# Passages between phases done by halves of the tokens, without GpSimd

## The chip, the cores and the metric

One core of a Trainium2 chip. The metric is the device time of one execution in microseconds (us). Five engines work in parallel, each through its own queue in order: TensorE (PE, matmul), VectorE (DVE), ScalarE (ACT), GpSimd (POOL) and SyncE (SP), which only issues DMAs here. They wait for each other through semaphores.

## The reference

A two-layer trunk over 544 tokens: 512 of a prompt and 8x4 of decoding samples, model width 1024. Cut to what matters:

```
def rms_norm(x, g):
    return x * rsqrt(mean(x * x, axis=-1) + EPS) * g

for l in range(DEPTH):                       # DEPTH = 2
    h = rms_norm(x, norm_mix_pre[l])
    if l % 2 == 0: mix = mixer_ab(h, ...)    # short convolution and window attention
    else:          mix = mixer_c(h, ...)     # HGRN2: gated recurrence, 8 heads
    x = x + rms_norm(mix, norm_mix_post[l])
    h = rms_norm(x, norm_ffn_pre[l])
    fo = (gelu(dwconv(h @ w_a)) * (h @ w_b)) @ w_down
    x = x + rms_norm(fo, norm_ffn_post[l])
```

So behind every mixer and every FFN two norms follow each other, over all 1024 channels: the statistics of the phase's output, the residual add, the statistics of the new x, and the scaled h that the next projection multiplies.

## The kernel before

Channels lie on the 128 partitions: x, h and the phase output (`mix`) are 8 tiles (`KD`) of 128 channels by 544 tokens. A PSUM accumulator (`acc[0]`, `acc[1]`) holds one output tile as two halves of 272 tokens (`H`). Each product is made in three passes: each weight and each activation is split into a high and a low part (`w_hi`, `w_lo`, `h_hi`, `h_lo`), and hi·hi, hi·lo, lo·hi are added.

There are eight phases in `PHASES`: in_ab, out_ab, up0, down0, in_c, out_c, up1, down1. Each consists of units, a unit being the weights of one output tile (8 or 11 k-tiles; a tile of down takes two units of 11). A unit's raw weights come by DMA from SyncE into one of four buffers; ScalarE casts each half of a unit to `w_hi`, VectorE subtracts to get `w_lo` (both in functions named `split`), into one of two slots. So a split of a unit waits until TensorE has done the unit two before it (`half_done`).

The order of work is written out by hand, one program for each engine; loops run over units. What a passage from one phase to the next does, in the order of the data:

- TensorE: `last_half` does the last half of the last output tile one token half after the other; `stats` multiplies sums of squares by a matrix of ones, which gives the sum over channels on every partition; `first_pair` does the first two units of the next phase k by k, as h tiles arrive, and then the statistics of the new x.
- VectorE: `last_out` copies the tile from PSUM to `mix`; `boundary` multiplies `mix` by the root (`S[3]`, L1252), adds it to x with the gain (L1257), and makes `h_lo` (L1064), two tiles behind the x update.
- ScalarE: squares (L721, L826 to L835), `norm_root` (Ln, then Exp with scale -0.5: L705, L707), and `normed`: `h_hi` (L713) and the square of the new x for each tile.
- GpSimd: `add_squares` multiplies the odd tiles of `mix` by the root (L1555), and adds the squares of the tiles one after the other into `S[2]` (L1561, L1571).

The root of the new x isn't needed before the matmuls: h is x times the gain, and the root (`rstd`) is multiplied into the unit's output behind them. So the next phase's first matmuls wait for h, and the first use of their output waits for `rstd`.

In `boundary` of ScalarE for the passage down0 to in_c the constants of mixer C are loaded (L852) and the recurrence's first state (L853). VectorE waits for all four constants before `head(0, None, 0)` of in_c, which begins with the copies of the first two accumulators. TensorE's third unit goes into the first accumulator and waits for that copy.

## Time and profile before

| | us |
|---|---|
| median of 3 runs | 1464.04 (1463.32 to 1465.4) |
| profiled execution, its own time | 1466.36 |
| its span, first to last instruction | 1464.6 |
| TensorE busy (PE) | 1386.5, 95% |
| TensorE weight loads (PEld) | 1352.5, 92% |
| VectorE busy (DVE) | 838.6, 57% |
| ScalarE busy (ACT) | 579.6, 40% |
| GpSimd busy (POOL) | 301.9, 21% |
| mean granted TensorE clock | 0.968 |

The busy share of an engine says how much it has to do over the whole span, not whether it holds the others up. TensorE has the most; of the chain of work that ended last it holds 79%, VectorE 11%. A granted clock of 1.00 is 2.4 GHz, 0.50 is 1.2 GHz. Matmuls overlap in their pipeline, so that the distance from one start to the next is shorter than one's duration.

### The profile page before, as it was taken

Reading aid. Unit: us, or ns where it says so; the run is one execution under the profiler, and the core shown is the slowest. Engines: PE = TensorE matmul, PEld = TensorE weight load, DVE = VectorE, ACT = ScalarE, POOL = GpSimd, SP = SyncE. Lnnn points to the kernel's source line nnn. Section 1 sums busy time; section 2 is a strip of 40 time slices with the busy share of each in tenths; the row PEclk is TensorE's granted clock in tenths of the full one; section 3 lists DMA queues with packets and bytes.
Section 4 is the critical chain, followed back from the end, with each engine's and each line's share of the span. In section 5 each row is a group of like instructions: output and inputs, shape, how many; then the busy total and the mean of one; then the engine's idle time right before and its main releaser. Section 6 shows DMA issues by size and latency. Waiting matters only on the chain.

```text
span 1464.6 us, 27604 instructions
## 1 busy us (share of the span) xinstructions
PE 1386.5 (95%) x10588; PEld 1352.5 (92%) x10588; DVE 838.6 (57%) x1287; ACT 579.6 (40%) x1110; POOL 301.9 (21%) x397
## 2 busy tenths in 40 slices
PE   9899997999999999977999999999699999999995
PEld 8887896999999999977999999989699999999995
DVE  6356538665555632258677777754865666562224
ACT  5235334433333322235555655543443333332221
POOL 2123215111111100033222222222411111120002
PEclk9979998999999999988999999999899999999998
DMA  7311130232222332231222222213132222233211
GB/s 266 95 39 58 50 96 30 88 100 86 86 86 86 113 98 81 72 96 44 89 87 75 88 88 88 72 49 101 32 98 86 86 86 86 86 113 112 82 37 61
DMA packets 38527, 123.32 MB, mean 84 GB/s; under 512 B 4105, under 2 KB 9865, under 8 KB 38345
## 3 DMA queue, kind: packets, MB, share of 16 engines
q1 hardware_dynamic: 31888, 110.74, 23.7%
q10 hardware_dynamic: 6408, 11.38, 2.1%
q8 instruction: 38, 0.62, 0.2%
q0 software_dynamic: 176, 0.44, 0.1%
q14 instruction: 17, 0.13, 0.0%
HBM read 113.98 MB, written 8.57 MB: 84 GB/s over the span
## 4 chain that ended last, share of the span: by engine, by line
PE 79%; DVE 11%; issue 4%; ACT 3%; ACTq 1%; DMA 0%; DVEq 0%; SPq 0%
PE acc L365 70%; PE aux L577 2%; DVE x L1257 2%; DVE w_lo L1056 1%; DVE mix L1252 1%; PE aux L619 1%; PE acc L383 1%; DVE lev L1354 1%; DVE h_lo L1064 1%; DVE scratch L1457 1%; PE aux L591 1%; PE aux L487 1%; DVE lev L1348 1%; PE aux L467 1%; ACT w_hi L693 1%
## 5 line engine op out<-in xcount | busy, mean ns | idle before, releaser
L1056 DVE TENSOR_TENSOR w_lo<-raw,w_hi 128x512 fp32r<-128x512 f32 (+1 forms) x372 | 313.4, 845 | 407.9 <-ACT w_hi L693 407.1
L365 PE MATMUL acc<-h_hi,w_hi 128*128 128x272 f32 x2208 | 475.5, 297 | 37.2 <-DVE h_lo L1064 33.6
L365 PE MATMUL acc<-h_hi,w_lo 128*128 128x272 f32 x2208 | 463.9, 292 | 0.0
L365 PE MATMUL acc<-h_lo,w_hi 128*128 128x272 f32 x2208 | 463.1, 292 | 0.0
L365 PEld LDWEIGHTS acc<-h_hi,w_hi 128*128 128x128 f32 x2208 | 354.6, 193 | 48.0 <-issue 27.4
L693 ACT CAST w_hi<-raw 128x512 fp32r<-128x512 f32 (+1 forms) x372 | 238.3, 643 | 386.7 <-PE acc L365 373.4
L365 PEld LDWEIGHTS acc<-h_lo,w_hi 128*128 128x128 f32 x2208 | 355.1, 193 | 0.0
L365 PEld LDWEIGHTS acc<-h_hi,w_lo 128*128 128x128 f32 x2208 | 352.2, 193 | 0.0
L365 PE MATMUL acc<-g_hi,w_lo 128*128 128x272 f32 x684 | 141.6, 288 | 0.0
L365 PE MATMUL acc<-g_hi,w_hi 128*128 128x272 f32 x684 | 141.4, 288 | 0.0
L365 PE MATMUL acc<-g_lo,w_hi 128*128 128x272 f32 x684 | 141.0, 288 | 0.0
L365 PEld LDWEIGHTS acc<-g_hi,w_hi 128*128 128x128 f32 x684 | 107.5, 188 | 0.0
L365 PEld LDWEIGHTS acc<-g_lo,w_hi 128*128 128x128 f32 x684 | 107.5, 189 | 0.0
L365 PEld LDWEIGHTS acc<-g_hi,w_lo 128*128 128x128 f32 x684 | 106.7, 189 | 0.0
L1561 POOL TENSOR_TENSOR scratch<-scratch 128x544 f32<-128x544 f32 x40 | 59.9, 1498 | 211.7 <-ACT scratch L826 195.8
L1648 POOL TENSOR_TENSOR scratch<-scratch,rstd 128x544 f32<-128x544 f32 x44 | 59.9, 1362 | 169.3 <-ACT scratch L884 169.3
L884 ACT ACTIVATE scratch<-scratch 128x544 f32<-128x544 f32 x44 | 29.0, 659 | 112.2 <-DVE scratch L1077 112.2
L890 ACT CAST g_hi<-scratch 128x544 f32 (+1 forms) x44 | 28.5, 647 | 98.0 <-DVE scratch L1307 93.7
L1589 POOL COPY sp<-st_f 128x16 f32 (+1 forms) x44 | 8.8, 200 | 256.1 <-DVE scratch L1301 243.1
L880 ACT ACTIVATE scratch<-scratch,vec 128x544 f32<-128x544 f32 x44 | 33.0, 750 | 65.7 <-DVE scratch L1301 64.0
L365 PE MATMUL acc<-y_hi,w_hi 128*128 128x272 f32 x240 | 51.1, 295 | 1.7 <-DVE y_lo L1462 1.6
L1309 DVE TENSOR_TENSOR g_lo<-scratch,g_hi 128x544 f32 (+1 forms) x42 | 30.5, 726 | 38.3 <-ACT g_hi L890 38.3
(247 smaller groups left out, 1621.5 us busy)
## 6 DMA issues: line engine op xcount, KB each, us to landing
raw<-in_w_up SPq DMA_DIRECT2D x88, 512.0 KB, 3.5
raw<-in_w_down SPq DMA_DIRECT2D x32, 704.0 KB, 4.1
raw<-in_w_in_c SPq DMA_DIRECT2D x32, 512.0 KB, 3.5
raw<-in_w_in_ab SPq DMA_DIRECT2D x18, 512.0 KB, 3.6
raw<-in_w_out_ab SPq DMA_DIRECT2D x8, 512.0 KB, 3.5
S<-in_state ACTq DMA_DIRECT2D x8, 512.0 KB, 4.1
o_ss<-Snew ACTq DMA_DIRECT2D x8, 512.0 KB, 2.6
raw<-in_w_out_c SPq DMA_DIRECT2D x8, 512.0 KB, 3.5
```

The lines of the kernel that those rows point to most:

```text
L365: mm = pe.matmul(acc[out][:, t, 0:H], w[slot][:, cols], mv[:, kk_, t * H:(t + 1) * H], start=start and k == 0 and q == 0, stop=stop and k ...
L383: mm = pe.matmul(acc[1][:, t, 0:H], w[n % 2][:, cols], mv[:, kt_base + k, t * H:(t + 1) * H], start=False, stop=k == kts - 1 and q == 2)
L577: mm = pe.matmul(out, lhs[:, c * CH:c * CH + rows], moving, start=True, stop=True)
L693: act.copy(w_hi[n % 2][:, h_ * HALF:h_ * HALF + kts * P], raw[n % 4][:, cols]).then_inc(hi_ready, 1)
L880: act.activation(S[1][:], S[0][:], ACT.Copy, scale=vec[:, bass.ds(w + u + 2 * i, 1)]).then_inc(tap_ready, 1)
L884: act.activation(S[2][:], S[1][:], ACT.Gelu_apprx_tanh).then_inc(act_done, 1)
L890: act.copy(g_hi[:, u + 2 * i, :], S[3][:]).then_inc(g_hi_ready, 1)
L1056: dve.tensor_tensor(w_lo[n % 2][:, to], raw[n % 4][:, cols], w_hi[n % 2][:, to], ALU.subtract).then_inc(lo_ready, 1)
L1257: dve.scalar_tensor_tensor(x[:, k, :], mix[:, k, :], col(pg, k), x[:, k, :], ALU.mult, ALU.add).then_inc(x_new, 1)
L1309: dve.tensor_tensor(g_lo[:, j, :], S[3][:], g_hi[:, j, :], ALU.subtract).then_inc(g_ready, 1)
L1561: pool.tensor_tensor(S[2][:], S[2][:], S[e][:], ALU.add).then_inc(sq_added, 1)
L1648: pool.tensor_tensor(S[2][:], S[2][:], rstd[:], ALU.mult).then_inc(gate_ready, 1)
```

## The change

At each of the four passages the work goes by halves of the tokens (272 each), half 0 first from end to end, then half 1:

- TensorE: the whole last output tile is done for half 0 and then for half 1 (`last_tile` for `last_half`), with the statistics of half 0 after four k of half 1. `first_pair` does both units for half 0, unit by unit in quarters, with the statistics of the output's half 1 after the first quarter, and then both units for half 1, k by k.
- The sums of squares of the new x are no longer added by an engine: ScalarE writes the 8 squares to a buffer of their own (`sq_up`, `sq_c`), TensorE adds them with 32 output rows at four places (`square_sums`), ScalarE copies the result to `S[2]` (`sums_out`), and one more matmul adds the four places (`pre_stats`). For half 1 this stands within the third unit (`third_unit`).
- VectorE makes all multiplies of `mix`, and `h_lo` one tile behind the x update instead of two. `last_out` of half 1 and the weight splits of the next phase's first units stand inside the passage.
- GpSimd has no work in a passage; it still adds the squares of the output tiles 0 to 6.
- The loads of mixer C's constants stand behind the last square instead of ahead of the first `h_hi`.
- SyncE stores the result in 16 halves instead of 8 tiles.

VectorE's queue at the passage out_ab to up0, before (`mix<-acc` are the copies of the last tile, `x<-` the residual update):

```order
L1229 COPY mix<-acc 128x272 x2
L1056 TENSOR_TENSOR w_lo<-raw,w_hi 128x512
L1252 TENSOR_TENSOR mix<-mix,scratch 128x544
L1257 SCALAR_TENSOR_TENSOR x<-mix,vec,x 128x544 x2
L1252 TENSOR_TENSOR mix<-mix,scratch 128x544
L1064 SCALAR_TENSOR_TENSOR h_lo<-x,vec,h_hi 128x544
L1257 SCALAR_TENSOR_TENSOR x<-mix,vec,x 128x544
L1064 SCALAR_TENSOR_TENSOR h_lo<-x,vec,h_hi 128x544
L1257 SCALAR_TENSOR_TENSOR x<-mix,vec,x 128x544
```

The same engine and place now:

```order
L1335 COPY mix<-acc 128x272
L1362 TENSOR_TENSOR mix<-mix,scratch 128x272
L1365 SCALAR_TENSOR_TENSOR x<-mix,vec,x 128x272
L1335 COPY mix<-acc 128x272
L1362 TENSOR_TENSOR mix<-mix,scratch 128x272
L1171 SCALAR_TENSOR_TENSOR h_lo<-x,vec,h_hi 128x272
L1365 SCALAR_TENSOR_TENSOR x<-mix,vec,x 128x272
L1162 TENSOR_TENSOR w_lo<-raw,w_hi 128x512
L1362 TENSOR_TENSOR mix<-mix,scratch 128x272
L1171 SCALAR_TENSOR_TENSOR h_lo<-x,vec,h_hi 128x272
L1365 SCALAR_TENSOR_TENSOR x<-mix,vec,x 128x272
```

The second copy stands behind the first x update, a weight split follows the second one, and each `h_lo` stands between the next tile's multiply and its x update.

ScalarE's queue at the passage down0 to in_c, before, from the second root on (`keep`, `masks`, `mask_s` and `own` are the four constants):

```order
L707 ACTIVATE scratch<-scratch 128x272
L852 DMA masks<-in_c_masks 128x640
L852 DMA mask_s<-in_c_mask_s 32x32
L852 DMA own<-in_c_own 96x1024
L852 DMA keep<-in_c_keep 128x544
L853 DMA S<-in_state 128x1024
L713 ACTIVATE h_hi<-x,vec 128x544
L721 ACTIVATE scratch<-x 128x544
```

And now, at the end of the same passage:

```order
L940 ACTIVATE h_hi<-x,vec 128x272
L958 ACTIVATE sq_c<-x 128x272
L962 DMA keep<-in_c_keep 128x544
L962 DMA masks<-in_c_masks 128x640
L962 DMA mask_s<-in_c_mask_s 32x32
L962 DMA own<-in_c_own 96x1024
L963 DMA S<-in_state 128x1024
L789 COPY scratch<-aux 128x272
```

The five loads moved from ahead of the first `h_hi` to behind the last square, ahead of the copy of the second half's sums.

The diff, cut to its core:

```diff
# TensorE
-            def last_half(m, moving, kt_base):
-                n, half_, _, kts = half_of(m)
-                pe.wait_ge(lo_ready, m + 1)
+            def last_tile(units, moving, norm):
                 for t in range(2):
-                    for k in range(kts):
-                        cols = slice(half_ * HALF + k * P, half_ * HALF + (k + 1) * P)
-                        for q, (w, mv) in enumerate([(w_hi, moving[0]), (w_hi, moving[1]), (w_lo, moving[0])]):
-                            mm = pe.matmul(acc[1][:, t, 0:H], w[n % 2][:, cols],
-                                           mv[:, kt_base + k, t * H:(t + 1) * H],
-                                           start=False, stop=k == kts - 1 and q == 2)
-                    mm.then_inc((cols_done, half_done)[t], 1)
+                    seen = 0
+                    for i, n in enumerate(units):
+                        base = 0
+                        for h_ in range(2):
+                            kts = half_of(2 * n + h_)[3]
+                            for k in range(kts):
+                                first, last = i + h_ + k == 0, (i, h_, k) == (len(units) - 1, 1, kts - 1)
+                                half(2 * n + h_, 0, 1, moving, (KFH * i if kts > 4 else 0) + base, first, last, ks=[k],
+                                     signal=int(t == 1 and k == kts - 1), ts=(t,), done=cols_done if last and not t else None)
+                                seen += 1
+                                if t == 1 and seen == 4:
+                                    stats(norm, 0)
+                            base += kts
...
+                pre = norm // 2
+                pe.wait_ge(evac, TILE0[name] - 1)
+                for e in range(2):
+                    for u in range(2):
+                        if (e, u) == (0, 1):
+                            pe.wait_ge(mix_cols, pre)
+                        for k in range(4):
+                            half(m + 2 * u + e, 0, u, h, 4 * e, e == 0, e == 1, half_ready(pre, 0) if u == 0 else None,
+                                 ks=[k], signal=0, ts=(0,))
+                        if (e, u) == (0, 0):
+                            stats(norm - 1, 1)
+                square_sums(pre, 0)
+                pe.wait_ge(evac, TILE0[name])
                 for k in range(8):
                     e = k // 4
                     for u in range(2):
-                        half(m + 2 * u + e, 0, u, h, 4 * e, e == 0, e == 1, tile_ready(norm // 2) if u == 0 else None,
-                             ks=[k % 4], signal={(0, 3): 1, (0, 7): 1, (1, 7): 2}.get((u, k), 0))
-                stats(norm)
+                        half(m + 2 * u + e, 0, u, h, 4 * e, e == 0, e == 1, half_ready(pre, 1) if u == 0 else None,
+                             ks=[k % 4], signal={(0, 3): 1, (0, 7): 1, (1, 7): 2}.get((u, k), 0), ts=(1,))
+                    if k == 4:
+                        pre_stats(pre, 0)
+                square_sums(pre, 1)
...
+            def third_unit(name, pre):
+                m = 2 * (UNIT0[name] + 2)
+                pe.wait_ge(evac, TILE0[name] + 1)
+                half(m, 0, 0, h, 0, True, False, ks=[0, 1], signal=0)
+                pre_stats(pre, 1)
+                half(m, 0, 0, h, 0, False, False, ks=[2, 3])
+            def square_sums(pre, t):
+                sq = sq_c if pre == 2 else sq_up
+                pe.wait_ge(rstd_ready, 4 * pre - 2 + t + 1)
+                for k in range(KD):
+                    j = k % 4
+                    pe.wait_ge(sq_pre, x_count(pre, t, k))
+                    mm = pe.matmul(A[2 + t][32 * j:32 * j + 32, 0:H], ones[:, 0:32], sq[:, k, cols(t)],
+                                   start=k < 4, stop=k >= 4)
+                mm.then_inc(sq_summed, 1)
+            def pre_stats(pre, t):
+                pe.wait_ge(sums_taken, 2 * pre - 1 + t)
+                pe.matmul(A[2 + t][:, 0:H], ones[:], S[2][:, cols(t)], start=True, stop=True).then_inc(stat_done, 1)
...
# ScalarE
+                last_out(post, 0)
+                norm_root(post, S[3], 0)
+                pre = (post + 1) // 2
+                if pre == 4:
+                    last_out(post, 1)
+                    norm_root(post, S[3], 1)
+                    return
+                m = 2 * UNIT0[name]
+                sq = sq_c if pre == 2 else sq_up
+                if pre == 2:
+                    split(m, 0)
+                for t in range(2):
+                    for k in range(KD):
+                        act.wait_ge(x_new, x_count(pre, t, k))
+                        c = gain_col(pre_kind, layer) + k
+                        act.activation(h_hi[:, k, cols(t)], x[:, k, cols(t)], ACT.Copy, scale=vec[:, c:c + 1]
+                                       ).then_inc(h_hi_ready, 1)
+                        if pre == 2 and (t, k) == (0, 0):
+                            split(m + 1, 0)
+                        if (t, k) == (0, 3 if pre == 2 else 0):
+                            last_out(post, 1)
+                        if (t, k) == (0, 4 if pre == 2 else 1):
+                            split(m + 2, 0)
+                        if (t, k) == (0, 5 if pre == 2 else 2):
+                            split(m + 3, 0)
+                        if (t, k) == (0, 5):
+                            norm_root(post, S[3], 1)
+                        if (t, k) == (1, 2):
+                            sums_out(pre, 0)
+                        if (t, k) == (1, 5):
+                            norm_root(2 * pre, rstd, 0)
+                        if (t, k) == (1, 6):
+                            split(m + 4, 0)
+                        act.activation(sq[:, k, cols(t)], x[:, k, cols(t)], ACT.Square).then_inc(sq_pre, 1)
...
-                    for to, table in ((masks, "c_masks"), (mask_s, "c_mask_s"), (own, "c_own"), (keep, "c_keep")):
+                    for to, table in ((keep, "c_keep"), (masks, "c_masks"), (mask_s, "c_mask_s"), (own, "c_own")):
                         act.dma_start(to[:], dram[table]).then_inc(const_c, 16)
                     act.dma_start(S0[:], dram["state0"][0, :, :, :]).then_inc(state0_in, 16)
-                pre = (post + 1) // 2
-                if pre == 4:
-                    return
-                normed(pre, gain_col(pre_kind, layer), name, lambda k: act.wait_ge(x_new, KD * (pre - 1) + 1 + k))
+                sums_out(pre, 1)
...
# VectorE
-            def boundary(post, layer, pre_kind=None, pre_layer=None, name=None):
-                dve.wait_ge(rstd_ready, 2 * (post + 1))
+            def boundary(post, layer, u_done, pre_kind=None, pre_layer=None, name=None):
                 pre = (post + 1) // 2
                 pg = gain_col(MIX_POST if post % 4 == 1 else FFN_POST, layer)
-                def lo(k):
+                last_out(u_done, pre, 0)
+                m = 2 * UNIT0[name] if pre < 4 else 2 * UNITS
+                at = {1: {(0, 0): "cols", (0, 1): 2, (0, 2): 3, (1, 6): 4},
+                      2: {(0, 0): 1, (0, 3): "cols", (0, 4): 2, (0, 5): 3, (1, 6): 4},
+                      3: {(0, 0): "cols", (0, 1): 2, (0, 2): 3, (1, 6): 4}, 4: {(0, 6): "cols"}}[pre]
+                def lo(t, k):
                     if pre < 4 and k >= 0:
-                        h_lo_tile(pre, k, gain_col(pre_kind, pre_layer))
-                for k in range(KD):
-                    if k % 2 == 0:
-                        step.mark(dve.tensor_tensor(mix[:, k, :], mix[:, k, :], S[3][:], ALU.mult))
-                    else:
-                        dve.wait_ge(mix_scaled, KD // 2 * (pre - 1) + 1 + k // 2)
-                    lo(k - 2)
-                    step.wait(dve)
-                    dve.scalar_tensor_tensor(x[:, k, :], mix[:, k, :], col(pg, k), x[:, k, :], ALU.mult, ALU.add
-                                             ).then_inc(x_new, 1)
-                lo(KD - 2)
-                lo(KD - 1)
-                if pre < 4:
-                    split(2 * UNIT0[name] + 4, 0)
-            out_phase("out_ab", 1)
-            boundary(1, 0, FFN_PRE, 0, "up0")
+                        h_lo_tile(pre, k, gain_col(pre_kind, pre_layer), t)
+                for t in range(2):
+                    dve.wait_ge(rstd_ready, 2 * post + 1 + t)
+                    if pre == 2 and t == 0:
+                        split(m, 0)
+                    for k in range(KD):
+                        step.mark(dve.tensor_tensor(mix[:, k, cols(t)], mix[:, k, cols(t)], S[3][:, cols(t)], ALU.mult))
+                        lo(t, k - 1)
+                        step.wait(dve)
+                        dve.scalar_tensor_tensor(x[:, k, cols(t)], mix[:, k, cols(t)], col(pg, k), x[:, k, cols(t)],
+                                                 ALU.mult, ALU.add).then_inc(x_new, 1)
+                        todo = at.get((t, k))
+                        if todo == "cols":
+                            last_out(u_done, pre, 1)
+                        elif todo is not None:
+                            split(m + todo, 0)
+                    lo(t, KD - 1)
...
# GpSimd
-            def add_squares(norm, post=False):
-                def scale(i):
-                    k = 2 * i + 1
-                    pool.tensor_tensor(mix[:, k, :], mix[:, k, :], S[3][:], ALU.mult).then_inc(mix_scaled, 1)
...
+            def add_squares(norm):
+                i = (norm + 1) // 2
+                if norm:
+                    pool.wait_ge(stat_done, 2 * norm)
+                pool.wait_ge(sq_ready, KD * i + 2)
+                pool.tensor_tensor(S[2][:], S[0][:], S[1][:], ALU.add).then_inc(sq_added, 2)
+                for k in range(2, KD - 1):
+                    pool.wait_ge(sq_ready, KD * i + 1 + k)
+                    pool.wait_ge(sq_added, (KD - 1) * i + k)
+                    pool.tensor_tensor(S[2][:], S[2][:], S[k % 2][:], ALU.add).then_inc(sq_added, 1)
```

## Rows read from the trace of the kernel before

**Rows 1.** TensorE's waits: for whom, us in total, times, longest.

```profile
PE acc L365 <- DVE h_lo L1064: 33.6, 13, 7.2
```

**Rows 2.** Stretches: from:to, length, busy us (count) by engine, clock, DMA.

```profile
225.60:257.20 31.60, 20.66 (x114) 18.99 (x113) 28.05 (x27) 14.82 (x26) 17.16 (x10) 0.78 0.05 17
...
241.60:245.00 3.40, 2.31 (x10) 2.31 (x11) 3.40 (x3) 0.55 (x1) 2.23 (x2) 0.50 0.00 0
```

**Rows 3.** Timeline, TensorE, out_ab to up0: start us, us, operation, [idle <-releaser].

```profile
219.71 0.41 PE L365 MATMUL acc<-y_hi,w_hi 128*128 128x272 f32 x2
...
222.72 0.29 PE L383 MATMUL acc<-y_hi,w_hi 128*128 128x272 f32 x1
...
242.69 0.82 PE L365 MATMUL acc<-h_hi,w_hi 128*128 128x272 f32 x2 [3.07 <-DVE h_lo L1064]
...
255.60 1.99 PE L409 MATMUL aux<-scratch,ones 128*128 128x272 f32 x8
257.23 0.61 PE L365 MATMUL acc<-h_hi,w_hi 128*128 128x272 f32 x2
...
276.40 0.51 PE L365 MATMUL acc<-h_hi,w_hi 128*128 128x272 f32 x2 [0.76 <-DVE scratch L1307]
```

**Rows 4.** Timeline, VectorE, out_ab to up0.

```profile
224.44 0.44 DVE L1229 COPY mix<-acc 128x272 f32<-128x272 f32 x1
...
248.16 1.87 DVE L1257 SCALAR_TENSOR_TENSOR x<-mix,vec,x 128x544 f32<-128x544 f32 x1
...
250.65 0.77 DVE L1257 SCALAR_TENSOR_TENSOR x<-mix,vec,x 128x544 f32<-128x544 f32 x1
251.35 0.77 DVE L1064 SCALAR_TENSOR_TENSOR h_lo<-x,vec,h_hi 128x544 fp32r<-128x544 f32 x1
252.56 1.37 DVE L1064 SCALAR_TENSOR_TENSOR h_lo<-x,vec,h_hi 128x544 fp32r<-128x544 f32 x1 [0.44 <-ACT h_hi L713]
```

**Rows 5.** Timeline, ScalarE, out_ab to up0.

```profile
224.97 0.43 ACT L833 ACTIVATE scratch<-mix 128x272 f32<-128x272 f32 x1 [1.38 <-DVE mix L1229]
...
227.38 0.49 ACT L705 ACTIVATE scratch<-aux,eps 128x272 f32<-128x272 f32 x1
...
228.74 0.43 ACT L707 ACTIVATE scratch<-scratch 128x272 f32<-128x272 f32 x1
...
245.10 0.64 ACT L721 ACTIVATE scratch<-x 128x544 f32<-128x544 f32 x1
...
250.72 0.60 ACT L693 CAST w_hi<-raw 128x512 fp32r<-128x512 f32 x1
...
251.79 0.73 ACT L713 ACTIVATE h_hi<-x,vec 128x544 fp32r<-128x544 f32 x1
...
258.53 0.43 ACT L707 ACTIVATE rstd<-rstd 128x272 f32<-128x272 f32 x1
```

**Rows 6.** Timeline, TensorE, in_ab: the sample scores, 32 output rows at four places.

```profile
52.84 0.66 PE L440 MATMUL aux<-kc,qbd 128*32 128x132 f32 x16
```

**Rows 7.** Chain that ended last: start us, us, what; the last tiles of down0, down1.

```profile
639.71 3.79 PE acc L383 x30
...
1442.28 3.78 PE acc L383 x30
```

**Rows 8.** Timeline, VectorE: the last `h_lo` ahead of in_c, and the last x updates.

```profile
670.09 1.38 DVE L1064 SCALAR_TENSOR_TENSOR h_lo<-x,vec,h_hi 128x544 fp32r<-128x544 f32 x1 [0.44 <-ACT h_hi L713]
...
1460.61 1.48 DVE L1257 SCALAR_TENSOR_TENSOR x<-mix,vec,x 128x544 f32<-128x544 f32 x2
```

**Rows 9.** Timeline, ScalarE's queue of DMAs, down0 to in_c.

```profile
646.26 0.38 ACTq L852 DMA_DIRECT2D masks<-in_c_masks  x1
...
647.62 0.45 ACTq L852 DMA_DIRECT2D keep<-in_c_keep  x1
```

**Rows 10.** DMA issues from 640 to 680: size, median us to landing.

```profile
raw<-in_w_in_c SPq DMA_DIRECT2D x2, 512.0 KB, 3.4
...
keep<-in_c_keep ACTq DMA_DIRECT2D x1, 272.0 KB, 5.9
```

247 lines of the change are left out of this document (121 added, 126 removed).

## The prediction

> **What bounds the kernel now.** I read the page first: it has TensorE busy nearly throughout, so time is lost or won only where it waits. The list of TensorE's waits comes next: the largest is for `h_lo`, 33.6 us in 13 waits [rows 1]. The timeline places them at the three passages between phases, out_ab to up0, down0 to in_c and out_c to up1, which are alike. In the view by stretches the first, from the end of the last output tile to the third unit of the next phase, is 31.6 us with 20.7 us of TensorE busy at a mean clock of 0.78, while VectorE is busy for 28 [rows 2]. A fourth stretch, after the last output tile, ends the program. VectorE's chain sets all four. In what follows S is the start of the last output tile, 219.71 at the first passage [rows 3].
>
> The order of time there: both halves of the post-norm root are there at 229.17, so VectorE starts the residual pass at S+9.5, and ends its last `h_lo` at 253.93 (S+34.2) [rows 4, 5]. TensorE does the last k's 12 matmuls and the statistics until 257.2, and ScalarE has the pre-norm root at 258.96 (S+39.2) [rows 3, 5]. From that root hangs VectorE's chain (scaling, convolution, gate), and TensorE waits for it at 276.40 [rows 3]. So the passage is worth what the second root's time moves by. Its distance from the last `h_lo` is 5.0 us.
>
> **The change, part by part.**
>
> Prices. A 272-column matmul takes (222.72-219.71)/24 = 0.125 us [rows 3]. Going through the last tile half by half issues the same 48 or 132, each already with its own weight load, so that costs nothing. A statistics pass is (257.23-255.60)/8 = 0.20 us [rows 3]. VectorE's copy of half a tile took 0.44 us, and I take the half multiply at the same; the x update took 0.77 at 544 columns when nothing disturbed it, about 0.05 more than a multiply, so 0.49 for half [rows 4]. Back to back, each starts 0.08 before the last one ends (250.65 and 251.35). ScalarE's square took 0.64 for 544 columns and 0.43 for 272, so `h_hi` goes from 0.73 to 0.52 [rows 5]. An engine starts about 0.04 us after what it waited for (252.56 after 252.52) [rows 4, 5].
>
> Earlier start. The first half of the tile is done at S+3.0, copied and squared by S+4.2; TensorE reaches the statistics after four further k at S+4.5 and needs 0.8; Ln and Exp take 0.49+0.43 and some latency [rows 5]. VectorE begins at S+6.5, 3.0 us before S+9.5.
>
> GpSimd's work is gone. VectorE's slow instructions (1.87 us against 0.77 for the same form) fall to the short price [rows 4]. But GpSimd's four multiplies per passage become VectorE's.
>
> The round trip. `h_lo(k-1)` now stands between multiply k and x update k, one tile behind, where it was two. From the start of an x update: 0.49, 0.04, `h_hi` 0.52, 0.04, then `h_lo` may start; 0.41 later the next x update does. A step is 1.50 us, though VectorE works only 1.2 of it. Bounds for a step are 1.2 (ScalarE's answer hidden) and 1.6; I take 1.50, since each piece is a measured row. There are 14 such steps: 21.0 us.
>
> The splits. Three weight splits stand inside the pass (next unit 1 twice, unit 2 once). ScalarE casts after `h_hi(k)`, VectorE's subtraction waits for that, and `h_lo(k)` stands behind it: 0.49+0.04+0.44+0.60+0.04+0.61+0.36+0.41 = 3.0, so 1.5 more than a step; together 4.5. Before, one cast lay beside slow x updates. Ends: first multiply 0.5; from half to half no x update is left to hide the answer, 1.09 until `h_lo` starts, 0.41, and a multiply waited for, 0.5, so 2.0; the last answer and `h_lo` 1.09+0.49 = 1.6. ScalarE also stops for two roots in the middle, each waiting for TensorE: 1.0 in all. Sum 21.0+4.5+0.5+2.0+1.6+1.0 = 30.6, against 24.7 before. The last `h_lo` comes at S+6.5+30.6 = S+37.1, that is 2.9 us later.
>
> From there to the root: 6 matmuls 0.8, square sums, half of the third unit's first part 1.5, one statistics matmul 0.4, drain and root 1.1. The square sums use 32 output rows in four places. The 16 passes of 132 columns at 52.84 took 0.66 us together, less a single one's 0.28 in the end, so starts some 0.026 apart [rows 6]; for 272 columns 0.053, so 0.9 with a little for the switch. If they didn't overlap it would be 16x0.20 = 3.2. I take 0.9. Total 4.7 to 5.1, as before (5.0). So at full clock out_ab to up0 loses **3.0 us**, and out_c to up1, the same code, **3.0**.
>
> Down0 to in_c. Here the last tile has 132 matmuls. S is 639.71, where the tile's last 30 begin, less 102x0.125: 626.9 [rows 7]. The first half ends at S+8.3 and VectorE starts at S+11.9. It holds two more splits (2.6), so 33.2: last `h_lo` at S+45.1, before S+44.6 (671.47) [rows 8]. The splits' casts wait for the second half, but no longer than VectorE needs to get there. Then a new wait: ScalarE's loads of masks and tables are issued after the last square, and VectorE waits for all four before it may copy the first two accumulators, for which TensorE's third unit waits. The first was issued at 646.26, the last at 647.62 and landed 5.9 later, 7.3 after the first [rows 9, 10]. Between 4.8 (the last issue and a weight load's 3.4) and 7.3, I take 6.0, as fewer weight loads run beside them. Copies can start at S+45.0+6.0 = 51.0, the third unit at 51.7, the root at 51.7+1.5+0.4+1.1 = S+54.7; before S+49.6, 5.0 after the last `h_lo`. **Loss 5.1**, bounds 3.9 and 6.4; without this wait 0.5.
>
> The end. No `h_lo` there, so a step is 0.44+0.03+0.41 = 0.88. S = 1442.28-12.8 = 1429.5 [rows 7]; start S+11.9 = 1441.4, first half 7.0, so 1448.4. The second half's copy, square, statistics and root run to 1450.6; another 7.0 gives 1457.6, against 1462.09 [rows 8]. **Gain 4.4**. SyncE's 16 half-size stores go out within the steps.
>
> At full clock: 3.0+3.0+5.1-4.4 = +6.7.
>
> The clock. At split 4 in the second half, behind ScalarE's root, two `h_lo` stand 3.7 us apart; TensorE has 0.8 us of work in this. Before, a wait of 3.07 us that ended at 242.69 was followed by matmuls at the half level, 1.2 GHz (0.50 in 241.6 to 245.0) [rows 2, 3]. What then lies on the path (6 matmuls, sums, 12 matmuls, one statistics) is 3.6 us at full level, and as much again at half. I take 1.5 of it in each of two passages and 1.0 at in_c, where TensorE waits for tables: +4.0. Bounds: 0, and 20 if the passages ran at half level throughout: 3.6 behind the last `h_lo` and up to 4.6 inside, where 6 matmuls take 1.4 instead of 0.8 and ScalarE waits longer for each sum. Sum **+10.7**.
>
> The Trainium skill, "TensorE: Matmul & The Clock Gate", section "HAM oscillation — how this bites in real kernels", says that bursts with waits between them drop the array to half rate over and over. That speaks against feeding it 6 matmuls per step; by it alone the high end would be the likelier, by the rows only the stretch behind the long gap is.
>
> What else is touched costs nothing: the wait for stored outputs, long landed; the removed `sq_added` waits; 1 us more of statistics on TensorE, which waits there anyway. If that cover went, it would be 1 us per passage.
>
> **The rivals.**
> *A. The answer of ScalarE is hidden.* If the step is 1.2 and a split 0.6, a pass is 14x0.3+3x0.9 = 6.9 us shorter, three of them 20.7; with 6.7 this gives -14, **1450**. For it: VectorE is freed of all 1.8 us instructions. Against: the last `h_lo` of before started 0.04 after the end of its `h_hi` [rows 4, 5]. It decides where a step is under 1.35 us. The Trainium skill, "SBUF — State Buffer", section "Who interferes with whom", has the slow instructions blocked by GpSimd; by that rule alone, with nothing on the round trip, this is where it would go.
> *B. The clock stays full:* +6.7, **1471**. For it: steps of 1.5 us never leave TensorE idle for long but once.
> *C. Half level through the passages:* 8 us more in each of two and 4 in the third than B, 6.7+20 = +26.7, **1491**. For it, the rows at 0.50; against, the level came back before as soon as work was dense.
> *D. Tables land in time and the step is 1.4:* 4.6 and 4.2 less than the forecast, +1.9, **1466**.
> *E. The sums of squares don't overlap:* 2.3 per passage on the path, and ScalarE, which waits for the first sums, held 0.7 longer: 9 on top of the forecast, **1484**. Against it is the row of 0.66 [rows 6].
>
> **How the numbers follow.** The profiled execution took 1466.36 us for a span of 1464.6; the runs shown have the median 1464.04, 2.3 less, and I add the sum to that: 1474.7, **1475**. Chances: forecast 0.46 (own range 1468 to 1481), B 0.18, C 0.06, E 0.08, D 0.09, A 0.13. Low end 1461 leaves most of A out, high end 1487 most of C. A difference of 0.2% (2.9 us) is about what a measurement of this kernel can tell from no change. Slower by more: 0.46+0.18+0.06+0.08 = 0.78. Within: D, 0.09. Faster: 0.13.
>
> **What would show it.** VectorE's residual updates start 3 us earlier against the last tile, at regular distances of 1.5 us, with waits for `h_hi` before each `h_lo`; three gaps of about 3 us with `w_lo` in them; no VectorE instruction near 1.8 us; TensorE waiting for VectorE's copy at in_c, and VectorE for a DMA; the last store about 4 us earlier. Wrong if steps are 1.2 us, if the pre-norm root comes earlier than 39 us after S in the first passage, or if the copies at in_c wait for nothing.

## The result, and the profile after

| | before | after |
|---|---|---|
| median of 4 runs, us | 1464.57 (1463.32 to 1465.4) | 1475.81 (1472.97 to 1477.96) |
| ratio of after to before, 95% interval | | 1.0074 (1.0057 to 1.0092) |
| span of the profiled execution, us | 1464.6 | 1471.2 |

The changed kernel is 0.74% slower, 11.2 us. 1475 had been predicted. Its profiled execution took 1472.97 us, the shortest of its four.

From the list of TensorE's waits in the changed kernel (engine, tile and line, what it waited for: total, times, longest):

```profile
PE acc L383 <- DVE h_lo L1171: 31.3, 28, 2.8
PE acc L383 <- DVE scratch L1200: 3.0, 1, 3.0
```

The waits for `h_lo` are 2.3 us less in all than before [rows 1], but twice as many, and the longest is 2.8 us where it was 7.2. A new wait of 3.0 us has come, for `scratch L1200`, VectorE's copy of in_c's first unit.

The view by stretches, with the stretch of [rows 2]:

```profile
225.60:257.20 31.60, 20.41 (x120) 16.45 (x119) 22.60 (x52) 17.38 (x42) 0.00 (x0) 0.84 0.05 17
```

TensorE does as much as before (20.4 us against 20.7), GpSimd nothing, and VectorE is busy 22.6 us instead of 28.1. VectorE has won 5.5 us of work and hasn't ended earlier. The timeline of VectorE shows why (start, duration, instruction, then in brackets the idle time before it and who ended it); out_ab to up0, where S is now 219.11:

```profile
225.75 0.44 DVE L1362 TENSOR_TENSOR mix<-mix,scratch 128x272 f32<-128x272 f32 x1 [2.97 <-ACT scratch L784]
...
229.35 0.69 DVE L1162 TENSOR_TENSOR w_lo<-raw,w_hi 128x512 fp32r<-128x512 f32 x1 [1.09 <-ACT w_hi L769]
...
234.78 0.50 DVE L1171 SCALAR_TENSOR_TENSOR h_lo<-x,vec,h_hi 128x272 fp32r<-128x272 f32 x1 [0.24 <-ACT h_hi L940]
...
236.29 0.50 DVE L1171 SCALAR_TENSOR_TENSOR h_lo<-x,vec,h_hi 128x272 fp32r<-128x272 f32 x1 [0.24 <-ACT h_hi L940]
...
239.96 0.50 DVE L1171 SCALAR_TENSOR_TENSOR h_lo<-x,vec,h_hi 128x272 fp32r<-128x272 f32 x1 [0.90 <-ACT h_hi L940]
...
253.83 0.69 DVE L1162 TENSOR_TENSOR w_lo<-raw,w_hi 128x512 fp32r<-128x512 f32 x1 [1.94 <-ACT w_hi L769]
...
256.29 0.50 DVE L1171 SCALAR_TENSOR_TENSOR h_lo<-x,vec,h_hi 128x272 fp32r<-128x272 f32 x1 [0.59 <-ACT h_hi L940]
```

VectorE starts at S+6.6, not at S+9.5. Then a tile at which no split stands takes 1.51 us (from 234.78 to 236.29), and in each of these VectorE waits 0.24 us for ScalarE's `h_hi`. The longer waits are for `w_hi`, the casts of the weight splits (1.09, one more of 1.10, 1.94), and 0.90 us where ScalarE makes a root between two tiles. No instruction is slow any more: the 1.87 us of [rows 4] are gone. The last `h_lo` ends at 256.79, S+37.7.

On TensorE and ScalarE, first the statistics of the output's second half and the square sums of the first half, then what follows VectorE's last `h_lo`:

```profile
236.18 1.11 PE L475 MATMUL aux<-scratch,ones 128*128 128x272 f32 x2
237.09 1.11 PE L480 MATMUL aux<-scratch,ones 128*128 128x272 f32 x2
...
244.10 1.12 PE L462 MATMUL aux<-sq_up,ones 128*32 128x272 f32 x16
...
255.34 0.39 PE L383 MATMUL acc<-h_hi,w_hi 128*128 128x272 f32 x1 [2.79 <-DVE h_lo L1171]
256.84 0.47 PE L383 MATMUL acc<-h_hi,w_hi 128*128 128x272 f32 x1 [0.49 <-DVE h_lo L1171]
258.38 2.04 PE L462 MATMUL aux<-sq_up,ones 128*32 128x272 f32 x16
...
263.15 0.43 ACT L784 ACTIVATE rstd<-rstd 128x272 f32<-128x272 f32 x1
```

Eight square sums take 1.12 us in the first half and 2.04 in the second: some 1.5 us behind the 2.79 us wait the granted clock falls, and it is 0.50 from 258 to 260 us, the lower level, 1.2 GHz. The first half of the passage has such a stretch too: TensorE waits 1.77, 2.26 and 1.92 us for its first three tiles with six records of work between, and the granted clock is 0.50 from 230 to 240 us. The statistics at 236.18 lie in it; they end at 238.20, and ScalarE's second post-norm root, which makes VectorE wait the 0.90 us, waits 0.48 us for them. The pre-norm root is there at 263.58, S+44.5, where it was S+39.2 [rows 5].

Down0 to in_c, VectorE and ScalarE behind the last `h_lo` (which ends at 676.37), and TensorE's wait:

```profile
679.87 0.39 ACT L789 COPY scratch<-aux 128x272 f32<-128x272 f32 x1 [3.71 <-PE aux L462]
680.15 0.22 ACT L1030 ACTIVATE lb<-lb 128x16 f32<-128x16 f32 x1
...
680.40 0.17 DVE L1215 TENSOR_TENSOR lb<-lb 128x8 f32<-128x8 f32 x1 [4.03 <-ACT lb L1030]
...
681.93 0.72 DVE L1200 COPY scratch<-acc 128x544 f32<-128x544 f32 x1
...
682.76 0.49 PE L383 MATMUL acc<-h_hi,w_hi 128*128 128x272 f32 x2 [2.96 <-DVE scratch L1200]
```

VectorE's wait isn't ended by a DMA. It is ended by `lb L1030`, the exponential of mixer C's lower bounds, which stands in ScalarE's queue behind the copy of the square sums. VectorE then has eight small instructions on `lb` and copies only at 681.93. The last table, issued at 676.69 and 4.9 us on the way, is there at 681.6. So two things hold the copy back side by side, and they end 0.3 us apart.

At the end of the program the last x update, `1468.52 0.50`, ends at S+28.1 where it was S+32.6.

For all that follows, one measure is taken per passage, in each profiled execution: from the start of VectorE's copy of output tile 6 (S+0.2) to the end of the pre-norm root, and at the end of the program to the end of the last x update.

| | to up0 | to in_c | to up1 | end | sum against before |
|---|---|---|---|---|---|
| before | 39.05 | 49.53 | 39.00 | 32.54 | |
| after | 44.27 | 55.36 | 43.94 | 27.86 | +11.3 |

5.22 + 5.83 + 4.94 - 4.68 = 11.3, and the medians differ by 11.2. The two profiled spans differ by only 6.6, mainly because of a stretch that the change doesn't touch: from the root of in_c to output tile 6 of out_c the profiled execution of before took 346.04 us and that of after 342.24. In other kernels of this study, with the same code there, it was 342.0 to 346.2, so some 4 us of a single span are chance. The stretches from root to tile 6 in both feed-forward phases were 368.00 to 368.03 in every kernel. A column of this table is one execution and not exact either: e3_tables and e4_tables_bounds below leave the passages to up0 and up1 as they are and have up to 0.4 us more there.

### The profile page after: what moved, and what is told of

Its sections match the earlier page's. It is cut to its first block, busy times and chain, and to the rows that moved or that the text cites. A ratio compares the mean times of both kernels' runs of the same rounds, so it can differ in the third digit from the quotient of the medians.

```text
span 1471.2 us, 27885 instructions
## 1 busy us (share of the span) xinstructions
PE 1394.6 (95%) x10672; PEld 1348.0 (92%) x10672; DVE 827.6 (56%) x1391; ACT 590.0 (40%) x1164; POOL 243.1 (17%) x363
## 4 chain that ended last, share of the span: by engine, by line
PE 79%; DVE 12%; ACT 5%; issue 3%; ACTq 1%; DMA 0%; SPq 0%; POOL 0%; DVEq 0%
PE acc L383 69%; PE aux L650 2%; DVE w_lo L1162 2%; DVE x L1365 2%; DVE h_lo L1171 1%; ACT h_hi L940 1%; PE aux L692 1%; DVE mix L1362 1%; DVE lev L1463 1%; DVE scratch L1565 1%; ACT w_hi L769 1%; PE aux L664 1%; PE aux L558 1%; DVE lev L1457 1%; PE aux L538 1%
## 5 line engine op out<-in xcount | busy, mean ns | idle before, releaser
L383 PE MATMUL acc<-h_hi,w_hi 128*128 128x272 f32 x2208 | 484.5, 297 | 40.7 <-DVE h_lo L1171 31.3
L383 PE MATMUL acc<-h_hi,w_lo 128*128 128x272 f32 x2208 | 469.9, 291 | 0.0
L383 PE MATMUL acc<-g_hi,w_hi 128*128 128x272 f32 x704 | 153.1, 288 | 0.0
L383 PE MATMUL acc<-g_hi,w_lo 128*128 128x272 f32 x704 | 153.0, 289 | 0.0
L383 PE MATMUL acc<-g_lo,w_hi 128*128 128x272 f32 x704 | 152.3, 288 | 0.0
L383 PEld LDWEIGHTS acc<-g_hi,w_hi 128*128 128x128 f32 x704 | 113.4, 188 | 0.1
L383 PEld LDWEIGHTS acc<-g_hi,w_lo 128*128 128x128 f32 x704 | 112.7, 189 | 0.0
L1668 POOL TENSOR_TENSOR scratch<-scratch 128x544 f32<-128x544 f32 x25 | 35.1, 1403 | 197.1 <-ACT scratch L904 195.8
L383 PE MATMUL acc<-y_hi,w_hi 128*128 128x272 f32 x256 | 57.1, 294 | 1.7 <-DVE y_lo L1570 1.6
L383 PE MATMUL acc<-y_lo,w_hi 128*128 128x272 f32 x256 | 55.9, 290 | 0.0
```

The lines of the kernel that those rows point to most:

```text
L383: mm = pe.matmul(acc[out][:, t, 0:H], w[slot][:, wc], mv[:, kk_, t * H:(t + 1) * H], start=start and k == 0 and q == 0, stop=stop and k == ...
L1668: pool.tensor_tensor(S[2][:], S[2][:], S[k % 2][:], ALU.add).then_inc(sq_added, 1)
```

## The experiments

Each kernel ran beside the kernel before on one chip; the ratio is to that. The last four columns are those of the table above.

| kernel | median us | ratio to before (95%) | to up0 | to in_c | to up1 | end |
|---|---|---|---|---|---|---|
| after | 1475.81 | 1.0074 (1.0057 to 1.0092) | 44.27 | 55.36 | 43.94 | 27.86 |
| e1_lag2 | 1475.14 | 1.0063 (1.0046 to 1.0080) | 43.30 | 55.27 | 43.18 | 27.87 |
| e2_splits | 1462.60 | 0.9981 (0.9971 to 0.9992) | 38.91 | 52.40 | 38.90 | 27.88 |
| e3_tables | 1478.60 | 1.0092 (1.0075 to 1.0108) | 44.68 | 55.80 | 43.92 | 27.88 |
| e4_tables_bounds | 1472.22 | 1.0048 (1.0033 to 1.0063) | 44.65 | 51.59 | 44.29 | 27.85 |
| e7_warm | 1470.64 | 1.0039 (1.0025 to 1.0053) | 42.15 | 54.61 | 42.20 | 27.86 |
| f2_halves_all | 1452.95 | 0.9921 (0.9904 to 0.9937) | 37.51 | 46.10 | 37.49 | 27.85 |
| e5_tail | 1458.89 | 0.9959 (0.9945 to 0.9973) | 39.05 | 49.53 | 39.00 | 27.86 |
| e6_vec_mults | 1461.57 | 0.9975 (0.9964 to 0.9987) | 38.36 | 48.82 | 38.30 | 31.48 |
| n1_full_no_gpsimd | 1455.80 | 0.9935 (0.9918 to 0.9951) | 35.74 | 50.65 | 35.69 | 31.50 |
| f0_full_tail | 1453.83 | 0.9918 (0.9901 to 0.9934) | 36.89 | 47.81 | 37.37 | 27.85 |
| f1_full_tail_warm | 1452.11 | 0.9909 (0.9893 to 0.9926) | 36.29 | 46.75 | 36.22 | 27.86 |
| f3_sums_by_four | 1445.52 | 0.9866 (0.9850 to 0.9883) | 34.12 | 44.59 | 34.06 | 27.89 |

The kernel before, measured again beside them, had medians of 1464.6 to 1465.5. The first seven rows are the changed kernel and what was mended in it, the others the kernel before and parts of the change put into it.

**e1_lag2: the round trip.** `h_lo` stands two tiles behind instead of one.

```diff
-                        lo(t, k - 1)
+                        lo(t, k - 2)
 ...
-                    lo(t, KD - 1)
+                    lo(t, KD - 2)
+                    lo(t, KD - 1)
```

> The changed kernel, but h_lo stands two tiles behind the multiply instead of one, in all three passages. Theory (the round trip sets the step: 0.50 x update, 0.52 h_hi on ScalarE, 0.42 h_lo, two hand-overs, 1.51 us in the trace): undisturbed, VectorE's three instructions start 0.35, 0.41 and 0.42 us apart, so the step falls to 1.2 us. Nine of the fifteen steps stand at no split, and the wait at the root (0.90) goes too: 0.3 x 9 + 0.9 = 3.6 us less per passage if nothing else comes last, 11 us in all; half of that if ScalarE, which then does casts and roots within shorter steps, takes part of it back. Time about 1467, between 1464 and 1471. The last h_lo of the first passage ends at S+34 to S+36 instead of S+37.7. Rival (VectorE's own work or ScalarE's h_hi and squares set the step, and the 0.24 us waits are only where it shows): steps stay at 1.5, time 1475 +-1.

Measured: 1475.14, where 1464 to 1471 had been expected: 0.7 us less than the changed kernel, within the intervals. The sum of the columns says 1.8 us less. From the timeline, VectorE (DVE) and ScalarE (ACT) in the passage to up0:

```profile
235.76 0.49 DVE L1171 SCALAR_TENSOR_TENSOR h_lo<-x,vec,h_hi 128x272 fp32r<-128x272 f32 x1
...
236.94 0.49 DVE L1171 SCALAR_TENSOR_TENSOR h_lo<-x,vec,h_hi 128x272 fp32r<-128x272 f32 x1
...
239.21 0.49 ACT L782 ACTIVATE scratch<-aux,eps 128x272 f32<-128x272 f32 x1 [1.99 <-PE aux L480]
...
240.92 0.50 DVE L1171 SCALAR_TENSOR_TENSOR h_lo<-x,vec,h_hi 128x272 fp32r<-128x272 f32 x1 [1.90 <-ACT h_hi L940]
...
251.05 0.49 ACT L782 ACTIVATE rstd<-aux,eps 128x272 f32<-128x272 f32 x1 [1.84 <-PE aux L469]
...
253.26 0.69 DVE L1162 TENSOR_TENSOR w_lo<-raw,w_hi 128x512 fp32r<-128x512 f32 x1 [3.44 <-ACT w_hi L769]
```

The first half of the theory holds: the step is 1.18 us (235.76 to 236.94) and the 0.24 waits are gone, so the round trip did set it. The second half falls: most of the won time comes back in two lumps, 1.90 us instead of 0.90 and 3.44 instead of 1.94. At both, ScalarE stands in its own queue at a root, waiting for TensorE's statistics (1.99 and 1.84 us; 0.48 and 0.66 in the changed kernel). These matmuls stand behind those of a certain tile (the fourth of the first half, the fifth of the second), which wait for that tile's `h_lo`; and `h_lo` one place later comes 0.6 us later (from VectorE's start 9.6 against 9.0 for the fourth). So the passage has two bounds side by side: the steps, and a loop VectorE, TensorE, ScalarE, VectorE that closes at each root. Making one shorter gives little while the other stands (1.0 us of the 3.6 expected in the passage to up0).

**e2_splits: the waits at the splits.**

```diff
# ScalarE
-                        if (t, k) == (1, 5):
-                            norm_root(2 * pre, rstd, 0)
-                        if (t, k) == (1, 6):
-                            split(m + 4, 0)
+                        if (t, k) == (1, 5):
+                            split(m + 4, 0)
+                            norm_root(2 * pre, rstd, 0)
# VectorE: which split stands behind which (half, tile)
-                at = {1: {(0, 0): "cols", (0, 1): 2, (0, 2): 3, (1, 6): 4},
-                      2: {(0, 0): 1, (0, 3): "cols", (0, 4): 2, (0, 5): 3, (1, 6): 4},
+                at = {1: {(0, 0): "cols", (0, 2): 2, (0, 3): 3, (1, 6): 4},
+                      2: {(0, 0): 1, (0, 3): "cols", (0, 5): 2, (0, 6): 3, (1, 6): 4},
```

> The changed kernel, with VectorE's w_lo of the splits one tile later than ScalarE's cast (for the third unit's first half ScalarE casts one tile earlier). The waits for w_hi in the trace are 1.09, 1.10 and 1.94 us per passage. Theory (each split costs 1.5 us because VectorE waits for a cast that itself waits behind h_hi; 0.6 of it is VectorE's own work and stays): 4.1 us less per passage, less the 0.24 waits at h_hi that come back in those three steps (0.7): 3.4 per passage, 10 us in all, time about 1466 (1463 to 1469). Rival (ScalarE is the one that is late, and the same wait comes back at the next h_hi): under 1 us per passage, time 1473 to 1476. The w_hi waits vanish in both; the distance from VectorE's start to the last h_lo (30.5 us now in the first passage, 31.0 to its end) tells them apart.

Measured: 1462.60, 13.2 us less than the changed kernel (the table's columns: 13.4). That is the theory, and more than its 10 us. None of the three `w_lo` waits any more, for instance

```profile
229.20 0.50 DVE L1171 SCALAR_TENSOR_TENSOR h_lo<-x,vec,h_hi 128x272 fp32r<-128x272 f32 x1 [0.24 <-ACT h_hi L940]
230.03 0.68 DVE L1162 TENSOR_TENSOR w_lo<-raw,w_hi 128x512 fp32r<-128x512 f32 x1
```

and the last `h_lo` ends 33.6 us after the copy of tile 6, where it was 37.5: 3.8 us. The other 1.5 us of the 5.4 lie behind the last `h_lo` and are mostly the clock's: the longest wait in the second half is now 1.33 us, and the last square sums run at the full level:

```profile
254.30 1.12 PE L462 MATMUL aux<-sq_up,ones 128*32 128x272 f32 x16
```

The edit changes two things for the third split: VectorE's part comes a tile later, and ScalarE's cast now stands ahead of the root instead of behind it. What each is worth wasn't separated.

**e3_tables and e4_tables_bounds: the wait at in_c.** In e3 the block of five loads behind the last square is taken out, and inside the loop over tiles stands

```diff
+                        load = {(0, 6): (keep, "c_keep"), (0, 7): (masks, "c_masks"), (1, 0): (mask_s, "c_mask_s"),
+                                (1, 1): (own, "c_own")}.get((t, k)) if post == 3 else None
+                        if load:
+                            act.dma_start(load[0][:], dram[load[1]]).then_inc(const_c, 16)
```

The fifth load, the first state, is issued at tile 3 of the second half.

> The changed kernel, with the four constant tables and the first state issued by ScalarE between tiles 6 of the first half and 3 of the second half of the passage down0 to in_c, about 18 us earlier, instead of after the last tile. What the prediction held (VectorE waits for the tables, 4.6 us): the root of in_c comes 4.6 us earlier, time 1471. What the trace of the changed kernel says (VectorE's first wait behind the last h_lo is for the exponential of the lower bounds, which ScalarE runs behind its copy of the square sums; the tables land 0.3 us before VectorE asks): no change, 1475 to 1476, VectorE's copy L1200 of the first unit still 5.5 us after the end of the last h_lo. A third possibility: the five issues, 0.4 us each on ScalarE, lengthen the steps that they stand in, +0.5 to +2 us.

e4 has this and, in the phase in_ab:

```diff
# ScalarE, in_ab
+                if m == 8:
+                    act.wait_ge(C["lb_ready"], 1)
+                    act.activation(lb[:, 1:3, :], lb[:, 1:3, :], ACT.Exp).then_inc(C["lb_done"], 1)
# VectorE, in_ab
+                if m == 10:
+                    lower_bounds_b()
+                    step.wait(dve)
```

> As the run before, and the lower bounds' exponential and VectorE's nine small instructions are done in in_ab, long before. Nothing of in_c's opening is then left between the last h_lo and VectorE's copies of the first pair. Theory (the two waits lay beside each other, and each alone hides the other): VectorE copies as soon as the last matmuls of the pair are done, about 1.6 us after the last h_lo ends, so TensorE finds the third unit's accumulator free when its square sums end; in the changed kernel it waited 2.96 us there. Root of in_c 3 us earlier (up to 4.6 if the shorter wait keeps TensorE at its full clock), time 1471 to 1473. Rival (the first use of a table of functions, or the third unit's own split, is next in line): under 1 us, time 1475.

Measured: 1478.60 with the tables alone (no gain; its interval overlaps that of the changed kernel, so that it is slower by 2.8 us is not shown), and 1472.22 with both, 3.6 us less than the changed kernel. In e3 VectorE still stands at `lb` for 3.75 us, and the copy comes 5.3 us behind the last `h_lo` though the tables have long landed. In e4 the copy comes 0.8 us behind it:

```profile
675.63 0.50 DVE L1173 SCALAR_TENSOR_TENSOR h_lo<-x,vec,h_hi 128x272 fp32r<-128x272 f32 x1 [0.59 <-ACT h_hi L943]
676.97 0.72 DVE L1202 COPY scratch<-acc 128x544 f32<-128x544 f32 x1 [0.83 <-PE acc L383]
```

The passage is 3.8 us shorter. The bounds moved alone were not tried; by the changed kernel's trace I estimate a gain of 0.3 us, since the last table lands at 681.6.

**e7_warm: the clock.** `keep_warm(n)` issues n matmuls of 128 columns whose results nobody reads; here they stand where TensorE waits for `h_lo`, in the first half and in the second.

```diff
+                            if (e, u) == (0, 0):
+                                keep_warm((4, 8, 7, 2)[k])
 ...
+                    keep_warm({6: 10, 7: 2}.get(k, 0))
```

> The changed kernel, and in TensorE's program 4, 8, 7 and 2 extra matmuls of 128 columns into a bank that nobody reads stand ahead of the first half's tiles 0 to 3, and 10 and 2 ahead of the second half's tiles 6 and 7, where the engine waits for h_lo. 0.19 us each at the full clock by the first ones of the program (12 in 4.3 us at the lower level, 0.36 each). They fill 1.3 to 1.9 us of gaps of 2.3 to 2.8 us. Nothing else is changed. Theory (the clock drop behind the gap at the third unit's split costs 1.5 to 2 us per passage: square sums at 2.04 us instead of 1.12, and the last tiles' and the third unit's matmuls): granted clock at the full level from S+30 on, root 1.5 us earlier in up0 and up1, less in in_c where VectorE's wait stands behind it: 3 to 4 us, time 1472. Rival (the lower clock lies under VectorE's chain): 1475 +-1. If the extra matmuls are late for a tile, up to +1 per passage: 1477.

Measured: 1470.64, 5.2 us less than the changed kernel (columns: 4.6). The view by stretches, over the stretch of [rows 2]:

```profile
225.60:257.20 31.60, 25.71 (x191) 22.21 (x190) 22.60 (x52) 17.62 (x43) 0.00 (x0) 1.00 0.06 17
```

The statistics in the first half, VectorE's wait behind the root that needs them, and the last square sums:

```profile
236.66 0.62 PE L483 MATMUL aux<-scratch,ones 128*128 128x272 f32 x2
...
239.75 0.50 DVE L1174 SCALAR_TENSOR_TENSOR h_lo<-x,vec,h_hi 128x272 fp32r<-128x272 f32 x1 [0.30 <-ACT h_hi L943]
...
257.58 1.12 PE L465 MATMUL aux<-sq_up,ones 128*32 128x272 f32 x16
```

Work that nobody needs makes the kernel faster: the clock is at its full level throughout, VectorE is busy as long as it was (22.60 us), and the passages to up0 and up1 are 2.1 and 1.7 us shorter, in_c 0.8. Of the 2.1 us, 1.5 lie behind the last `h_lo` (5.3 us to the root instead of 6.8), and 0.6 in the first half, where VectorE waits 0.30 us at the root instead of 0.90. This is the prediction's clock term (4.0) measured by itself, though it had looked only at the second of these places.

**e5_tail: the end alone, in the kernel before.**

```diff
# SyncE, TensorE, ScalarE and VectorE for down1 as in the changed kernel; VectorE:
+                if post == 7:
+                    out_half(0)
+                    for t in range(2):
+                        q = slice(t * H, (t + 1) * H)
+                        dve.wait_ge(rstd_ready, 15 + t)
+                        for k in range(KD):
+                            step.mark(dve.tensor_tensor(mix[:, k, q], mix[:, k, q], S[3][:, q], ALU.mult))
+                            step.wait(dve)
+                            dve.scalar_tensor_tensor(x[:, k, q], mix[:, k, q], col(pg, k), x[:, k, q],
+                                                     ALU.mult, ALU.add).then_inc(x_new, 1)
+                            if (t, k) == (0, 6):
+                                out_half(1)
+                    return
```

> The kernel before, with only the end of the program done as in the changed kernel: the last output tile of down1, its statistics, root, scaling, x update and stores by halves of the tokens, all on VectorE. The three passages between phases stay as before. Theory (the end's gain is its own, and stands beside the losses of the passages): the last x update ends 4.5 us earlier, as in the changed kernel, time 1461 (1460 to 1462). Rival (sixteen stores of 136 KB instead of eight of 272 KB end later, or the earlier end owes something to what came before it): 0 to 2 us less, 1463 to 1465.

Measured: 1458.89, ratio 0.9959 (0.9945 to 0.9973), which is 4 to 8 us less. 1460 to 1462 had been expected, so the median gain is a little larger. The last x update is 4.7 us earlier. The end's gain is its own.

**e6_vec_mults: GpSimd's multiplies alone, in the kernel before.**

```diff
-                    if k % 2 == 0:
-                        step.mark(dve.tensor_tensor(mix[:, k, :], mix[:, k, :], S[3][:], ALU.mult))
-                    else:
-                        dve.wait_ge(mix_scaled, KD // 2 * (pre - 1) + 1 + k // 2)
+                    step.mark(dve.tensor_tensor(mix[:, k, :], mix[:, k, :], S[3][:], ALU.mult))
```

GpSimd's own four multiplies are taken out of `add_squares`.

> The kernel before, whole tiles everywhere, but GpSimd's four multiplies by the root per passage are VectorE's; GpSimd still adds the squares. One part of the change alone. Undisturbed, VectorE's three instructions of a tile take 2.1 us (starts 0.64, 0.70 and 0.70 apart); beside GpSimd each takes 1.1 us more. Theory (GpSimd's work costs VectorE more than it saves it): eight tiles take 16.8 us and six additions disturb for 1.1 to 1.8 us each, 24 to 26 us against 24.7: passages within 1 us of before. At the end, where no addition is left, 8 x 1.40 = 11.2 us against 13.0, 1.8 us less. Time 1461 to 1466. Rival (the multiplies on GpSimd were a real relief): 4 x 0.64 us more per passage, +7 in all, 1472.

Measured: 1461.57, 3.9 us less; each passage is 0.7 us shorter and the end 1.1. So what GpSimd did for VectorE cost VectorE more than it saved. Two rows of this kernel's timeline, the first beside one of GpSimd's remaining additions, the second where GpSimd rests:

```profile
244.68 1.88 DVE L1064 SCALAR_TENSOR_TENSOR h_lo<-x,vec,h_hi 128x544 fp32r<-128x544 f32 x1
...
248.91 0.77 DVE L1064 SCALAR_TENSOR_TENSOR h_lo<-x,vec,h_hi 128x544 fp32r<-128x544 f32 x1
```

The same instruction takes 1.88 us or 0.77. The Trainium skill, "SBUF — State Buffer", section "Who interferes with whom", gives VectorE and GpSimd one shared pair of ports under an exclusive lock; by that rule the slow ones are those that found it taken. The trace agrees: GpSimd's additions run from 243.50 to 247.76 us and from 250.28 to 251.64, and at 248.91 it rests.

**n1_full_no_gpsimd: the change without its halves.** Beside the edit of e6, GpSimd's additions of the pre-norm squares go too:

```diff
# ScalarE
-                    act.activation(S[k % 2][:], x[:, k, :], ACT.Square).then_inc(sq_ready, 1)
+                        act.activation((sq_c if pre == 2 else sq_up)[:, k, :], x[:, k, :], ACT.Square).then_inc(sq_pre, 1)
# TensorE, in first_pair, whole tiles
+                    if norm and k >= 6:
+                        square_sums(norm // 2, range(6) if k == 6 else (6, 7))
```

> The change without its halves: whole tiles through the passages and the end as in the kernel before, h_lo two tiles behind, but no GpSimd work between phases (multiplies on VectorE; the pre-norm's squares go to a buffer and TensorE adds them, six tiles ahead of the last matmuls and two behind). Theory (what the change lost, it lost by the halves: round trip one tile behind, three w_hi waits, twice as many hand-overs; what it gained by quieting GpSimd is hidden under that): VectorE starts at S+9.5, eight steps of 2.04 us and the last h_lo put its end at S+27 against S+34.2 before. Root 5.5 to 7 us later, S+33 to S+34 against S+39.2: 5 us less in up0 and up1 each, 3 less in in_c (the exponential of the lower bounds then comes last), and 1.8 less at the end. Time 1450 (1447 to 1455). Rival 1 (square sums on TensorE and the longer path from the last h_lo to the root eat it): root at S+38 or later, 1461 to 1465. Rival 2 (the halves are what helps, and GpSimd's going costs): above 1465.

Measured: 1455.80, 9.6 us less than before; 14 to 15 had been expected. VectorE does what was expected, steps of 2.03 us (from the start of one `h_lo` to the next) and the last `h_lo` 26.0 us after the copy of tile 6 (34.0 before). But the root comes 9.7 us behind that instead of 5.0. TensorE, which waited for VectorE in the kernel before, is now the late one:

```profile
234.83 0.79 PE L370 MATMUL acc<-h_hi,w_hi 128*128 128x272 f32 x2 [5.94 <-DVE h_lo L1111]
248.06 2.03 PE L417 MATMUL aux<-sq_up,ones 128*32 128x272 f32 x24
251.71 1.11 PE L417 MATMUL aux<-sq_up,ones 128*32 128x272 f32 x8
```

From 234.83 on it never waits again in the passage. In the passage to in_c TensorE waits the same 2.9 us behind the lower bounds as in the changed kernel, and the passage is longer than before (50.65 against 49.53).

**f0_full_tail and f1_full_tail_warm.** f0 is n1 with the end of e5, the lower bounds of e4 and the square sums spread over more places:

```diff
-                    if norm and k >= 6:
-                        square_sums(norm // 2, range(6) if k == 6 else (6, 7))
+                    if norm and k in (3, 5, 6, 7):
+                        square_sums(norm // 2, {3: (0, 1, 2), 5: (3, 4), 6: (5,), 7: (6, 7)}[k])
```

> Whole tiles through the three passages without GpSimd work (as n1_full_no_gpsimd), the end by halves (as e5_tail), the lower bounds' exponential and VectorE's nine small instructions done in in_ab, and TensorE's square sums spread: tiles 0 to 2 behind tile 3's matmuls, 3 and 4 behind tile 5's, 5 behind tile 6's, 6 and 7 behind tile 7's. n1_full_no_gpsimd left these: TensorE had 24 square-sum records in 2.03 us between tiles 6 and 7 while it was itself the late one, 2.9 us of waiting in in_c behind the lower bounds, and an end 3.6 us later than by halves. If they add up: 1455.8 - 3.6 (end) - 4 (in_c) - 1.5 to 2 per passage: 1443 (1440 to 1447). If TensorE stays late because its clock is half after the 5.9 us wait for the first h_lo, the spread sums give nothing: 1448.

f1 adds one line ahead of `first_pair`'s first wait:

```diff
+                    keep_warm(24)
```

> The run before with 24 extra matmuls of 128 columns into an unused bank ahead of TensorE's wait for the first h_lo of each passage (about 4.5 us of a 5.9 us wait). By e7_warm, which kept the full clock and took 1.7 to 2.1 us off the passages to up0 and up1: here TensorE is the late engine behind VectorE's last h_lo (root 9.7 us behind it in n1_full_no_gpsimd, 5.0 before), so the clock should be worth at least as much: 2 us per passage, 6 us below f0_full_tail. Rival (the clock has recovered by the middle of the passage anyway, and what is left is work at full clock): under 2 us in all.

Measured: 1453.83 and 1452.11. Both expectations were missed. In f0 the end gave 3.6 us and in_c 2.8, but up0 and up1 became 1.2 and 1.7 us longer. A full clock gave f1 only 1.7 us by the medians (columns: 2.8) where 6 had been expected, so there the rival holds. The reason is in TensorE's timeline of f0: spreading the sums made them dearer.

```profile
241.78 1.12 PE L445 MATMUL aux<-sq_up,ones 128*32 128x272 f32 x12
246.02 1.11 PE L445 MATMUL aux<-sq_up,ones 128*32 128x272 f32 x8
248.75 1.10 PE L445 MATMUL aux<-sq_up,ones 128*32 128x272 f32 x4
251.49 1.11 PE L445 MATMUL aux<-sq_up,ones 128*32 128x272 f32 x8
```

Three tiles, two and one: all cost the same 1.1 us. Together 4.4 us where n1 had 3.1.

**f3_sums_by_four.**

```diff
-                    if norm and k in (3, 5, 6, 7):
-                        square_sums(norm // 2, {3: (0, 1, 2), 5: (3, 4), 6: (5,), 7: (6, 7)}[k])
+                    if norm and k in (5, 7):
+                        square_sums(norm // 2, {5: (0, 1, 2, 3), 7: (4, 5, 6, 7)}[k])
 ...
-                half(m, 0, 0, h, 0, True, False, ks=[0, 1], signal=0)
+                half(m, 0, 0, h, 0, True, False, ks=[0], signal=0)
```

> As f1_full_tail_warm, but TensorE's square sums come in two groups of four tiles (0 to 3 behind tile 5's matmuls, 4 to 7 behind tile 7's) instead of four groups of three, two, one and two, and the third unit does the statistics behind its first tile instead of its second. In the traces so far a group took 1.10 us with one tile (4 records), 1.11 with two (8), 1.12 with three (12) and 2.03 with six (24). Theory (sums of up to four tiles, each in its own 32 columns of the array, run beside each other, so a group costs by its rounds of four, not by its passes): two groups of 1.1 us, 2.2 us less on TensorE, which is the late engine here; with the statistics 0.6 earlier the root comes 2.8 us earlier per passage, 8 us in all, time 1444 (1442 to 1447). Rival (the 1.1 us are the price of the passes, and a group of four takes 1.5 or more): time 1448 to 1450. If TensorE stops being the late one, it waits for the last h_lo and the gain ends there: 1446 to 1448.

Measured: 1445.52, ratio to before 0.9866 (0.9850 to 0.9883): 6.6 us less than f1, 19.8 less than the kernel before and 30 less than the changed one. The two groups:

```profile
245.13 1.12 PE L446 MATMUL aux<-sq_up,ones 128*32 128x272 f32 x16
249.39 1.12 PE L446 MATMUL aux<-sq_up,ones 128*32 128x272 f32 x16
```

Four tiles cost what one did in f0. The passages are 2.2 us shorter, of 2.8 expected: TensorE now waits for `h_lo` at tiles 4 and 5 too (0.35 and 0.20 us), which is the rest, so the third possibility holds in part. The root still comes 8.1 us behind the last `h_lo`.

**f2_halves_all: the halves with all of it mended.** The edits of e1, e2, e4 and e7 together, and the first half's pre-norm root behind the last square:

```diff
-                        if (t, k) == (1, 5):
-                            norm_root(2 * pre, rstd, 0)
 ...
+                norm_root(2 * pre, rstd, 0)
                 sums_out(pre, 1)
```

> The changed kernel by halves with everything that was found to cost in it mended: w_lo of the splits one tile later, tables and lower bounds early, h_lo two tiles behind, the pre-norm root of the first half behind the last square instead of in the passage, extra matmuls as in e7_warm. Single effects so far: splits 13.2, tables and bounds 3.6, clock 5.2 (part of it already in the splits' figure), h_lo two behind 0.7 while the splits and roots stood in its way. Theory (the halves lose only by these): steps of 1.2 us and last h_lo at S+32 or earlier, time 1450 to 1456, so still behind whole tiles without GpSimd work (n1_full_no_gpsimd with its end by halves would be 1452, and f0_full_tail less). Rival (a half costs by itself: twice the hand-overs, two roots on the way): it stops at 1459, where e2_splits and e4_tables_bounds add up to.

Measured: 1452.95, 22.9 us less than the changed kernel and 12.6 less than the kernel before, as expected: what made the change lose is these things. The last `h_lo` ends 29.6 us after the copy of tile 6. e2, e4 and e7 have 13.2, 3.6 and 5.2 us by themselves, 22 in all, but e2 and e7 share the clock's part, so `h_lo` two tiles behind and the moved root seem to be worth something here; they weren't measured alone.

But halves cost something by themselves as well. By whole tiles the last `h_lo` still comes 3.5 us earlier (26.06), and f3 ends 7.4 us below f2. An undisturbed pass over 16 half tiles takes VectorE 16 x 1.18 = 18.9 us, one over 8 whole tiles 8 x 2.03 = 16.2 (the steps of e1 and of n1). These 2.7 us nearly use up the 3.0 us by which the halves start earlier.

## Why the prediction was right, point by point

1475 was forecast and 1475.8 measured. In the passages to up0 and up1 and at the end the mechanism was largely the one forecast; at in_c it was another one, and that its size agreed was luck.

**VectorE's start** was forecast at S+6.5 and was at S+6.6. **GpSimd's quiet**: up to the last `h_lo` no VectorE instruction takes more than 0.69 us, as forecast, and e6 and n1 show that this helps by itself (3.9 and 9.6 us).

**The step** was forecast at 1.50 us and took 1.51, and e1 shows that the round trip makes it. What the prediction left out is that the step was not the only bound: with steps of 1.18 us the time hardly moves. Rival A (1450) rested on steps of 1.2 us and splits of 0.6. f2, which has both by its edits, and in_c and the clock mended besides, came to 1452.95; shorter steps alone, in e1, came to 1475.14.

**The splits** were counted at 1.5 us each over a step. The first two are 2.96 and 2.97 us from one x update to the next, 1.46 over a step. The third is 3.81 (x updates at 251.39 and 255.20), 0.8 more than was counted, since ScalarE's root stands ahead of the cast. The other root costs 0.7 (0.90 us of waiting instead of 0.24). The prediction had 1.0 us for both roots as a term of its own, so the sum nearly holds: the last `h_lo` ends at S+37.7, forecast S+37.1. e2 shows that the waits at the splits and what hangs on them were the largest thing in the loss: mending them gives 13.2 us where the whole loss was 11.2, and the changed kernel is then 2.8 us faster than before.

**From the last `h_lo` to the root** it was 6.8 us, where 4.7 to 5.1 at full clock and 1.5 for the lower level were forecast. The square sums were 1.12 us at the full level, forecast 0.9; rival E's 3.2 is out (even at the lower level they took 2.04).

**The clock**: +4.0 forecast, 5.2 by e7 (4.6 in its columns). Rival B (1471) assumed a full clock; e7 brings that about by its extra matmuls and takes 1470.64. Rival C, half level through the passages, is out: 0.84 was granted over the stretch. The place that the prediction named, behind the third unit's split, is where 1.5 of the 2.1 us in up0 lie. It had put nothing for the first half, but there the granted clock was 0.50 from 230 to 240 us, and that cost the other 0.6 through ScalarE's wait for the statistics. So a small piece of rival C's mechanism was there.

**Down0 to in_c**: here this part of the prediction failed, and only its size came out. The prediction said that VectorE waits for four tables, and that without this wait the loss is 0.5 at full clock. VectorE copied at S+50.5 (forecast S+51.0), but what it waited for last was `lb L1030`, which the new order had put behind the second half's square sums; the prediction had looked past `lower_bounds_b`, which stands ahead of the wait for the tables. By the prediction, early tables alone (e3) would have given 4.6 us, and they gave none; tables and bounds both early (e4) gave 3.8 us in the passage. The passage lost 5.8 us, where 5.1 + 1.0 were forecast. The two figures are so close because the last table lands only 0.3 us before VectorE is through with `lb`.

**The end**: a gain of 4.4 was forecast and 4.7 measured in the trace, and e5 shows it alone.

Sum: +4.5, +6.1, +4.5 and -4.4 forecast, +5.2, +5.8, +4.9 and -4.7 measured. What the parts of the change do is now clear: quieting GpSimd wins, halves at the end win, and halves in the passages lose, mostly by the order of the queues, and in part because two half instructions take longer than a whole one. Whether e5's 6.5 us by medians, against 4.7 in its trace, is more than chance stays open, and so does n1's 9.6 against 6.5.

## What to carry to other kernels

Where two engines hand tiles to and fro, a pass has several bounds beside each other (the step, and every place where an in-order queue stops for a third engine's result), and shortening one shows nothing until the others are moved too; price them together, and move the work that makes a queue stop (casts, roots, loads, small set-up instructions) a step away from its user. Work halved to start earlier also halves what each hand-over covers, and the halves together take longer than the whole (0.44 us twice against 0.72 for a multiply here). Before giving an idle engine work, look for the same instruction at two durations in the busy engine's rows.

## What was not expected of the hardware

- Sums into 32 columns of the array cost by rounds of up to four tiles of x, not by passes: with both halves of 272 tokens, 1.10 us for one tile (4 records), 1.11 for two, 1.12 for three and for four (16 records), 2.03 for six; with one half, 1.12 for eight. That is 0.5 to 0.56 us a round. The Trainium skill, "TensorEngine Tiling (Array Packing)", section "Key Properties", says that different tiles of the array can run their weight loads and matmuls in parallel; the trace agrees. A round with a lone tile costs as much as one with four.
- In the changed kernel waits of 1.77, 2.26 and 1.92 us, with three records of work behind each of the first two, went with a granted clock of 0.50 (230 to 240 us), and some 1.5 us behind the wait of 2.79 us it fell to 0.50 again. With 0.6 to 2.4 us of extra matmuls in each of the long waits it stayed at the full level (mean 0.84 without and 1.00 with them over the same stretch).
- With the same code there, the stretch from in_c's root to out_c's tile 6 takes 342.0 to 346.2 us from one execution to the next. In one part of it, 21 us long and with a wait of 1.6 us in it, the granted clock was 0.92 in the trace of before and 1.00 in that of after. Most of what spreads this kernel's runs over 4 us may lie there; this wasn't tested.
